# One PSUM accumulator for the three products of a split-precision weight block

## The reference

```
y = x @ w          # x: 256 tokens x 2048 (or 5632) features, w: float32, read once from memory
```

## Time and profile before

| | |
|---|---|
| median of 3 runs | 3703.81 us |
| the runs | 3722.18, 3690.02, 3703.81 us |
| profiled execution: span from first to last instruction | 3721.3 us |
| the run of those shown that lies nearest to that span | 3722.18 us |
| TensorE, matmuls, busy in the span | 3336.9 us (90%), 18334 instructions |
| TensorE, weight loads | 2861.2 us (77%), 18334 instructions |
| VectorE | 2198.9 us (59%) |
| ScalarE | 1572.3 us (42%) |
| GpSimd | 211.8 us (6%) |
| mean granted TensorE clock | 0.938 of full |

### The profile page before, as it was taken

One profiled execution on the slowest core, in us unless ns is written; L12 is line 12 of the kernel. 1 busy time (PEld: TensorE's weight loads), 2 busy tenths in 40 slices (PEclk: granted clock), 3 DMA queues, 4 the chain that ended last, 5 costly groups with the idle time before them and its releaser, 6 DMA issues.

```text
span 3721.3 us, 49866 instructions
## 1 busy us (share of the span) xinstructions
PE 3336.9 (90%) x18334; PEld 2861.2 (77%) x18334; DVE 2198.9 (59%) x2263; ACT 1572.3 (42%) x1863; POOL 211.8 (6%) x89
## 2 busy tenths in 40 slices
PE   6996598799999997999999988985688999999966
PEld 5885486688888886788888876864467888888855
DVE  5555575666666456556555456575666555555466
ACT  3443353444544433444444333445334444443333
POOL 1000120200000001000000001000110000000011
PEclk9997798899999999999999998987799999999978
DMA  5662154366666554555665654642145666655533
GB/s 170 211 187 82 45 159 136 110 188 185 185 185 185 187 186 138 163 185 185 196 190 188 193 178 122 186 136 81 46 147 153 185 185 185 184 188 186 186 104 108
DMA packets 321784, 595.23 MB, mean 160 GB/s; under 512 B 18228, under 2 KB 41940, under 8 KB 321684
## 3 DMA queue, kind: packets, MB, share of 16 engines
q1 hardware_dynamic: 313808, 587.27, 50.8%
q10 hardware_dynamic: 7876, 6.63, 0.6%
HBM read 591.70 MB, written 2.13 MB: 160 GB/s over the span
## 4 chain that ended last, share of the span: by engine, by line
PE 85%; DVE 10%; issue 2%; ACT 1%; DMA 1%; POOL 0%; POOLq 0%; DVEq 0%; ACTq 0%; SPq 0%
PE acc L421 54%; PE acc L423 27%; DVE OPR L1202 2%; DVE wl L1111 1%; DVE T L1217 1%; DVE X L1222 1%; ACT wh L745 0%; PE acc L393 0%; PE acc L460 0%; DVE S L1190 0%; DMA raw<-in_w_in 0%; DVE T L1125 0%; PE acc L584 0%; DVE S L1261 0%; PE acc L482 0%
## 5 line engine op out<-in xcount | busy, mean ns | idle before, releaser
L421 PE MATMUL acc<-OPR,wh 128*128 128x512 f32 x6480 | 2324.6, 403 | 129.6 <-DVE OPR L1202 84.2
L1111 DVE TENSOR_TENSOR wl<-raw,wh 128x1024 fp32r<-128x1024 f32 x1112 | 1403.6, 1270 | 1266.8 <-ACT wh L745 1266.0
L423 PE MATMUL acc<-OPR,wl 128*128 128x256 f32 x6480 | 1832.4, 283 | 0.0
L745 ACT ACTIVATE wh<-raw 128x1024 fp32r<-128x1024 f32 x1112 | 1167.7, 1058 | 1511.4 <-PE acc L423 1487.1
L421 PEld LDWEIGHTS acc<-OPR,wh 128*128 128x128 f32 x6480 | 1239.9, 191 | 448.6 <-issue 102.5
L423 PEld LDWEIGHTS acc<-OPR,wl 128*128 128x128 f32 x6480 | 1244.8, 192 | 0.0
L421 PE MATMUL acc<-HR,wh 128*128 128x512 f32 x2272 | 798.6, 397 | 3.3 <-DVE T L1125 2.3
L423 PE MATMUL acc<-HR,wl 128*128 128x256 f32 x2272 | 635.3, 280 | 0.0
L421 PEld LDWEIGHTS acc<-HR,wh 128*128 128x128 f32 x2272 | 426.6, 188 | 108.2 <-DVE T L1125 2.9
L423 PEld LDWEIGHTS acc<-HR,wl 128*128 128x128 f32 x2272 | 428.3, 189 | 0.0
L1125 DVE TENSOR_TENSOR T<-acc,T 128x1024 f32<-128x1024 f32 (+1 forms) x111 | 134.4, 1211 | 14.1 <-ACT T L763 14.0
(11 more groups left out here) (257 smaller groups left out, 1274.5 us busy)
## 6 DMA issues: line engine op xcount, KB each, us to landing
raw<-in_w_up SPq DMA_DIRECT2D x176, 512.0 KB, 3.9
raw<-in_ff_w_gate SPq DMA_DIRECT2D x176, 512.0 KB, 3.7
raw<-in_ff_w_up SPq DMA_DIRECT2D x176, 512.0 KB, 4.5
raw<-in_ff_w_down SPq DMA_DIRECT2D x176, 512.0 KB, 4.4
raw<-in_w_in SPq DMA_DIRECT2D x170, 512.0 KB, 3.7
raw<-in_w_down SPq DMA_DIRECT2D x88, 512.0 KB, 4.7
raw<-in_w_out SPq DMA_DIRECT2D x64, 512.0 KB, 4.5
raw<-in_w_ple_gate SPq DMA_DIRECT2D x32, 512.0 KB, 3.8
```

The lines of the kernel that those rows point to most:

```text
L421: pe.matmul(acc[:, b + t, :], wh[:, s, col:col + P], x, start=(u == 0 and k == 0), stop=False)
L423: mm = pe.matmul(acc[:, b + t, 0:T], wl[:, s, col:col + P], x[:, 0, :], start=False, stop=last)
L745: act.activation(wh[:, s, :], raw[:, s, :], ACT.Copy).then_inc(hi_done, 1)
L1111: dve.tensor_tensor(wl[:, s, :], raw[:, s, :], wh[:, s, :].bitcast(F32), ALU.subtract)\
```

## The change

The three products go to one accumulator of 256 columns, as three matmuls of 256 moving columns. A tile then takes half a bank, two tiles share one (so that only the first matmul into the bank carries the start flag), a block takes 2 banks, and two blocks alternate between banks 0, 1 and 2, 3. T1, take and collect go. Whoever used collect's result now reads the accumulator itself, and VectorE waits for the block's last matmul (function finished) and not for ScalarE. Several semaphores that stood for the second instruction are replaced by `acc_free`. The norms' sums always go to bank 7.

```diff
+        STAT = acc[:, 7, 0:T]
+        def acc_tile(g, t):
+            return acc[:, 2 * (g % 2) + t // 2, T * (t % 2):T * (t % 2 + 1)]
+        def acc_tiles(g, n):
+            return acc[:, 2 * (g % 2):2 * (g % 2) + 2, :].rearrange("p b (c t) -> p (b c) t", t=T)[:, 0:n, :]
...
+            def triple(dst, w_hi, w_lo, x, first, last):
+                pe.matmul(dst, w_hi, x[:, 0, :], start=first, stop=False, skip_group_check=True)
+                pe.matmul(dst, w_hi, x[:, 1, :], start=False, stop=False, skip_group_check=True)
+                return pe.matmul(dst, w_lo, x[:, 0, :], start=False, stop=last, skip_group_check=True)
...
-                                pe.matmul(acc[:, b + t, :], wh[:, s, col:col + P], x,
-                                          start=(u == 0 and k == 0), stop=False)
-                                mm = pe.matmul(acc[:, b + t, 0:T], wl[:, s, col:col + P], x[:, 0, :],
-                                               start=False, stop=last)
+                                mm = triple(acc_tile(g, t), wh[:, s, col:col + P], wl[:, s, col:col + P], x,
+                                            u == 0 and k == 0 and t % 2 == 0, last)
...
-                act.activation(T1[:, 0:tiles, :], acc[:, b:b + tiles, T:2 * T], ACT.Copy).then_inc(t1_full, 1)
...
-            def collect(ph, c, i, dst, tiles=4):
-                g = ph["c0"] + c
-                dve.wait_ge(t1_full, i * 2 + (g + 1))
-                b = 4 * (g % 2)
-                dve.tensor_tensor(dst, acc[:, b:b + tiles, 0:T], T1[:, 0:tiles, :], ALU.add).then_inc(acc_free, 1)
+            def finished(ph, c, i):
+                dve.wait_ge(units_used, i * (2 * ph["upc"]) + (ph["u0"] + (c + 1) * ph["upc"]))
...
-                    collect(ph, c, i, T2[:, 0:tiles, :], tiles)
-                    collected(ph, c, i)
-                    dve.tensor_tensor(HFc[:, bass.ds(i * 8 + (first + 4 * c), tiles), :], T2[:, 0:tiles, :],
-                                      bc(rstd[:, :], tiles), ALU.mult).then_inc(done, 1)
+                    finished(ph, c, i)
+                    dve.tensor_tensor(HFc[:, bass.ds(i * 8 + (first + 4 * c), tiles), :],
+                                      acc_tiles(ph["c0"] + c, tiles), bc(rstd[:, :], tiles), ALU.mult)\
+                       .then_inc(acc_free, 1)
...
+            def residual(ph, c, i):
+                finished(ph, c, i)
+                x = X[:, bass.ds(i * 8 + 4 * c, 4), :]
+                dve.tensor_tensor(x, acc_tiles(ph["c0"] + c, 4), x, ALU.add).then_inc(acc_free, 1)
+            def to_y(y, first):
                 def evac(ph, c, i):
+                    finished(ph, c, i)
+                    dve.tensor_copy(y[:, bass.ds(i * 8 + (first + 4 * c), 4), :], acc_tiles(ph["c0"] + c, 4))\
+                       .then_inc(acc_free, 1)
```

More of the change, by code:

```diff
@@ L262, in program @@
                ("ff1", 16), ("mixp", 16), ("nsa", 16), ("ff2", 16), ("ple", 16), ("p", 1)]
-        SRC = {n: 4 * i for i, n in enumerate(["cross", "ffn", "final", "ff1_pre", "mix_pre", "ff2_pre",
-                                               "ple_pre"])}
+        SRC = {n: 4 * i for i, n in enumerate(["ff1_pre", "mix_pre", "ff2_pre", "ple_pre"])}
+        XSRC = {"cross": "w_out", "ffn": "w_co", "final": "down"}
         XS = {}
@@ L442, in _ @@
             pe.wait_ge(cst_loaded, 16)
-            pe.wait_ge(proj_out, 12)
+            pe.wait_ge(acc_free, blocks("w_in", 12))
             for n in range(8):
@@ L510, in _ @@
             pe.wait_ge(acc_free, PH["w_cq"]["c0"])
-            stat("cross", colsum, bank=stat_bank(PH["w_cq"]))
-            pe.wait_ge(proj_out, 15)
+            stat("cross", colsum)
+            pe.wait_ge(acc_free, blocks("w_cq", 1))
             for n in range(2):
@@ L650, in _ @@
                     x = OPR[:, h, :, :]
-                    pe.matmul(acc[:, 4 * (g % 2) + t, :], wh[:, s, h * P:(h + 1) * P], x, start=True, stop=False)
-                    mm = pe.matmul(acc[:, 4 * (g % 2) + t, 0:T], wl[:, s, h * P:(h + 1) * P], x[:, 0, :],
-                                   start=False, stop=True)
+                    mm = triple(acc_tile(g, t), wh[:, s, h * P:(h + 1) * P], wl[:, s, h * P:(h + 1) * P], x,
+                                t % 2 == 0, True)
                 if c % 2:
@@ L814, in _ @@
             gemm("w_in", bias_tiles, norm="mix")
-            act.wait_ge(proj_out, 12)
+            act.wait_ge(acc_free, blocks("w_in", 12))
             def q_rev(h):
@@ L967, in _ @@
                     if c == 2 and u == 2:
-                        act.wait_ge(proj_out, 23)
+                        act.wait_ge(acc_free, blocks("in_b", 2))
                     if c == 2 and 2 <= u < 6:
@@ L985, in _ @@
                     act.activation(TRIG, ANG, ACT.Sin).then_inc(trig_ready, 1)
-            act.wait_ge(proj_out, 25)
+            act.wait_ge(acc_free, blocks("in_b", 4))
             for j, w in enumerate((a["cmp_k_w2_2"], a["cmp_v_w2_2"])):
@@ L1419, in _ @@
             ff_up("up", 0, True, "ffn")
-            gemm("down", residual("final"))
-            dve.wait_ge(ssq_src, SRC["final"] + 4)
+            gemm("down", residual)
+            dve.wait_ge(acc_free, blocks("down", 4))
             fold("final", X[:, 12:16, :])
@@ L1724, in _ @@
             squares("mem", four(MEM), mem_loaded, 16, 0)
-            for name in ("cross", "ffn", "final", "ff1_pre"):
-                squares(name, four(X, n=3 if name == "final" else 4), ssq_src, SRC[name] + 1)
+            squares("cross", four(X), acc_free, blocks("w_out", 1))
+            squares("ffn", four(X), acc_free, blocks("w_co", 1))
+            squares("final", four(X, n=3), acc_free, blocks("down", 1))
+            squares("ff1_pre", four(X), ssq_src, SRC["ff1_pre"] + 1)
             squares("ff1_post", four(Y, n=3), acc_free, PH["ff1_down"]["c0"] + 1)
@@ L1739, in _ @@
             squares("ple_pre", four(X), ssq_src, SRC["ple_pre"] + 1)
-            squares("ple_post", four(HFc, 20, 3), y_done, 1)
+            squares("ple_post", four(HFc, 20, 3), acc_free, blocks("ple_proj", 1))
 MATRICES = ["w_in", "w_out", "w_cq", "w_ckv", "w_co", "w_up", "w_down", "ff1_w_gate_2", "ff1_w_up_2",
```

133 lines of the change are left out of this document (52 added, 81 removed).

## The result

The changed kernel takes 3786.74 us, median of four runs from 3782.39 to 3790.58, against 3701.35 us of the kernel before (3690.02 to 3722.18 in four runs). The ratio is 1.0216, with an interval of 1.0181 to 1.025: slower by about 2%. The profiled execution took 3787.63 us with a span of 3785.6. The profiled execution of before took 3722.18; from profile to profile the change costs 65.4 us, and from median to median 85.4, because that execution was the slowest of the four.

The account below looks back on a forecast made before the run. TensorE's streaming, plus its stops between stages, was taken to bound the kernel. 3722.2 us + 26 for pace - 17 for stops = 3731, less half of the profiled run's 18 above the median: 3722; range 3670 to 3762.

Parts of the forecast that it names:

- The failed step: TensorE's stream: a matmul of half the columns costs half, so three of 256 cost what 512 + 256 do.
- the compression's 0.118 a step: Twenty steps of 256-column matmuls in the compression, taken as the new stream's price: 0.354 us a triple, +26 us.
- the upper bound +52: TensorE's pace at most 0.119 us a step, from rounding in the compression's twenty steps: 0.357 a triple, +52 us.
- excess that goes with the columns: TensorE's pairs at 346 to 353 ns against the skill formula's 325, read as a cost by column.
- Rival (b): TensorE's stream: the weight load becomes the bound, 0.119 us a step or more; 3757 us at 0.357; chance 0.27.
- Rival (a): TensorE's stream: a triple runs like a pair, level by level; TensorE's term 0, median 3687 us; chance 0.3.
- Rival (c): Stage-end stops: evacuation worth more than counted, as shorter stops might keep TensorE's clock; chance 0.03.
- Nothing changes there: TensorE at the lower clock: a pair's 0.64 us is 768 columns at 1.2 GHz, no room for cost by instruction.
- The stops: TensorE's waits between stages shrink as copy and add go: 17 us less in all, bounds 8 and 24.
- In_b: End of stage in_b: the add and its handover go from the stop, 1.4 us less.
- If a stop appears in the middle of a stage: Sign of being wrong: TensorE stopping inside a stage, where it had no stop before; no size given.
- the half of the median's 18 us: Profiled run was 18 us above the median; half taken off in case triples draw their levels anew: 3731 to 3722.

Follow-up runs that it names:

- The stream alone: Kernel before with each TensorE pair replaced by three matmuls of 256 columns, the old copy and add kept: 3807.85 us, ratio 1.0252.

## Why the prediction was wrong

**The failed step** is the question "Is the cost by column or by instruction?" and its answer. It took the compression's 0.118 a step for the price of the new stream, 0.354 a triple. The forecast was +26 us for the pace and the upper bound +52 (0.357); with the prediction's own mean it was +79 (0.360), with the one read from start to start +77, outside. The stream alone made the whole loss, and the step had three faults.

The 0.23 and 0.11 of a pair were read as what each matmul costs. The runs with 512 + 512 and with one short matmul show that they aren't: a distance between starts doesn't say which neighbour is paid for. Measured in uniform streams, 512 columns take 226.7 ns and 256 take 120.0. With the operands where both kernels have them, the cost at full clock is the columns plus 13.3 ns an instruction, and the lower level of a pair is exactly the sum. One more matmul then costs 13.3 ns; from the lower level, all 8752 would be +117 us, and as 6064 pairs had already run at a level 6.7 ns worse, +76. The row that I used against a cost by instruction was the "excess that goes with the columns", at 346 to 353 for 320 of columns: with two instructions that excess is 2 x 13.3, and one form alone can't tell the two readings apart. The 13.3 is no constant of the chip. It is 10 in a stream of 256 with the weights 8 bytes off, where a triple at 350.0 costs less than a pair at its upper level; it is absent at the lower clock; and with 128 columns the floor of 108 to 113 stands in place of 53.3 + 13.3.

The Trainium skill, "TensorE: Matmul & The Clock Gate", section "Back-to-back issue gap", has a fixed cost for each warm matmul, and that is the kind that the runs show here; they disagree with its 2.5 ns, with 13.3 in the changed kernel and 10 at the best placement found. The section itself keeps that formula for a single matmul by itself, and says that in a stream with loads both operations set the distance, which I left out. I took the misfit in size as a reason to doubt the kind.

The compression's 0.118 was the nearest row in form. In the changed kernel it is still 118 ns, median of its steps at full clock, while the gemm's are 120.0. It is a stream of the same shape with its operands in other places, and the experiments show that moving operands can change the mean step between 116.7 and 120.0. That the places are what sets the compression's 118 was not tested. "0.119 at most" was a bound from the rounding of that one stream; nothing tied it to the places of another.

**Rival (b)** had the sign and the point from which it decides, 0.1185 a step, but its price stopped at 0.357. Its mechanism is half shown: with 128 columns a matmul still costs 108 to 113 ns, so there is a floor, most likely the load, just under the 256-column step of 116.7 to 120.0. That the load alone makes the 120 is not shown, since the step depends on where the operands lie. Rival (a) fell: no stretch of triples ran at 0.346, and in the changed kernel none at 0.353. Rival (c) did not come up.

**The lower clock.** "Nothing changes there" held: 0.640 both times. But it was no evidence against a cost by instruction: the same streams have it at full clock and not at the lower one.

**The stops** held as a sum, 17 forecast, 17.2 measured, 16.7 with the evacuation changed alone; in part by luck, since the items that were forecast came to 14.2 and the rest was in none of them. By item: w_in 1.4 and 1.39; w_cq 2.3 and 2.27; w_co 4.0 and 3.65; down 1.4 and 1.38; the last stage 4.5 and 4.6; the gates 1.9 and 0.9. In_b gave 0.05, not 1.4: TensorE waited there before for the add alone, since collect freed the banks ahead of the scaling, and now waits for the scaling in its place. An evacuation in one step frees the banks later than the first of two did. The stop between ple_gate and ple_proj, 1.5 us, was not in the sum and went; nor were the last 1.5, small differences over the span.

**What was missed:** the three stops at the jump back, 8.0 us of idle time. "If a stop appears in the middle of a stage" stood among what would make the prediction wrong, without a mechanism. Of the two signs of being wrong, this one and a pace outside 0.346 to 0.357, both came. The clue was in the change itself: the loop's body grows by half in TensorE's instructions. Afterwards the page shows more transfers of instructions, 120 packets for 62; the kernels with pairs have 62 or 63, those with triples throughout 115 or 120.

**The levels** were named and used rightly as the source of the spread before, and wrongly as something that the changed kernel would draw anew. It has one level, so the half of the median's 18 us that I took off was not there to take. The sum with the measured terms is 3722.2 + 77 - 2 - 17.2 + 8.0 = 3788, and the median is 3786.7.

## What to carry to other kernels

Take the price of a matmul from streams of one shape and count, never from the distance of two unlike neighbours. Splitting one matmul into two cost 13.3 ns against the pair's lower level and 6.7 against its upper one; with the weights 8 bytes off the triple, at 350.0, lay between the two. Under 256 columns little was left to save, 7 to 12 ns for half of the columns. An engine's copy and add beside a TensorE that never stops are worth only what they hold up at the ends of the stages: 260 us of them gave 17. Before one judges a change of 1 or 2% in such a stream, move the operands by some bytes and read the counts, and if a loop's body has grown, search for a stop where it jumps back.

## What the hardware showed that I had not expected

The same instructions have several fixed prices. A triple took 350.0, 353.3 or 360.0 ns, a pair 346.7, 351.1 or 353.3, constant through a stage. For triples the price changes when operands are moved in SBUF, and in one run, with x 8 bytes further, also from stage to stage. For pairs it changes from stage to stage too, and by the spread of the times from run to run of the same kernel: 8752 x 6.6 ns are 58 us, as much as the 57 between the fastest and the slowest of 60 runs of before. What in the places does it, and what draws the level, is open.

A jump back over 44 units of 24 matmuls and their loads stops TensorE for 2.4 to 2.9 us; over 44 units of 16 it didn't at all. Shown is only that the stop goes with the jump. A fetch of instructions would fit the 120 transfers for 62, but with the loop written out and the stops gone there are still 115, so the count doesn't decide it.

A matmul of 128 columns costs nearly what one of 256 does. The Trainium skill, "TensorE: Matmul & The Clock Gate", section "LDWEIGHTS", has 107 ns for 128 columns of weights; the floors of 108 and 113 ns at full clock, estimates from these runs, agree with it, but at the lower clock 213 are left for the short matmul, so what makes the floor goes with the clock. With two short matmuls in a triple the pace was that of the lower clock throughout, and 6145.58 us were needed for two thirds of the triples' columns.
